# Where weights and inputs start in SBUF: one ring slot and four input quarters at other residues of 256 bytes

## What is computed

```python
def layer(x, ...):
    h = rms_norm(x, g_pre_mix)
    qA, kA, vA, qB, kB, vB = split(h @ w_in)            # 2048 x 4352
    oA = sliding_window_gqa(rope(qA), rope(kA), vA)     # window 128, with sinks
    oB = dilated_attention(rope(qB), rope(kB), vB)      # (128,1), (512,4), (2048,16)
    o = concat(rms_norm(oA, g_out_a), rms_norm(oB, g_out_b))
    x = x + rms_norm(o @ w_out, g_post_mix)             # 2048 x 2048
    h = rms_norm(x, g_pre_ffn)
    u, up = h @ w_gate, h @ w_up                        # 2048 x 5632 each
    c = conv_b + sum(conv_w[j] * shifted(u, j) for j in range(3))
    return x + rms_norm((gelu(c) * up) @ w_down, g_post_ffn)   # 5632 x 2048
```

## The kernel before

| tensor | tile step in bytes | residue of its tiles |
|---|---|---|
| `wh`, `wl`, all four slots | 512 between weight tiles | 128 |
| `hh`, `hl` | 1280 (264 columns in rows of ROW = 320) | 128, all 16 |
| `oBh`, `oBl` | 1056 | 224 + 32 j for tile j |
| `gh` | 1056 | 128 + 32 kt |
| `gl` | 1056 | 0 + 32 kt |

## Time and profile before

### The profile page before, as it was taken

One profiled execution on the slowest core, in us unless ns is written; L12 is line 12 of the kernel. 1 busy time (PEld: TensorE's weight loads), 2 busy tenths in 40 slices (PEclk: granted clock), 3 DMA queues, 4 the chain that ended last, 5 costly groups with the idle time before them and its releaser, 6 DMA issues.

```text
span 1178.7 us, 25575 instructions
## 1 busy us (share of the span) xinstructions
PE 1154.6 (98%) x9947; PEld 1122.2 (95%) x9947; DVE 700.6 (59%) x1052; ACT 552.7 (47%) x857; POOL 108.0 (9%) x163
## 2 busy tenths in 40 slices
PE   8999999999999799999999999999999999999995
PEld 8999889988999799999999999999999999999994
DVE  6977565674475866665656565665656444454445
ACT  6545555565455654444445444444545333343331
POOL 0200111111002010010001001100100000020001
PEclk9999999999999899999999999999999999999998
DMA  9646676677555345555565555546455655555542
GB/s 330 194 148 229 236 254 235 218 232 237 170 178 180 108 146 194 190 183 187 162 204 170 185 179 184 186 164 207 167 194 176 211 178 178 179 181 180 180 156 73
DMA packets 60497, 222.21 MB, mean 189 GB/s; under 512 B 7064, under 2 KB 9312, under 8 KB 58336
## 3 DMA queue, kind: packets, MB, share of 16 engines
q1 hardware_dynamic: 56032, 196.53, 51.2%
q0 software_dynamic: 4272, 24.94, 6.4%
q10 hardware_dynamic: 144, 0.05, 0.0%
HBM read 216.45 MB, written 5.00 MB: 188 GB/s over the span
## 4 chain that ended last, share of the span: by engine, by line
PE 93%; DVE 4%; ACT 1%; DMA 1%; issue 0%; SPq 0%; DVEq 0%; ACTq 0%
PE ps L1138 29%; PE ps L1139 29%; PE ps L1140 29%; DVE wl L681 1%; PE ps L1311 1%; PE ps L1229 1%; PE ps L1292 1%; DMA raw<-in_w_in 1%; PE ps L1220 1%; PE ps L1218 1%; PE ps L1247 0%; PE ps L1165 0%; DVE yT L985 0%; DVE ps L984 0%; ACT oBh L545 0%
## 5 line engine op out<-in xcount | busy, mean ns | idle before, releaser
L1138 PE MATMUL ps<-hh,wh 128*128 128x264 f32 x2080 | 593.3, 285 | 7.9 <-DVE hl L894 5.8
L1140 PE MATMUL ps<-hh,wl 128*128 128x264 f32 x2080 | 586.8, 282 | 0.0
L1139 PE MATMUL ps<-hl,wh 128*128 128x264 f32 x1952 | 550.8, 282 | 0.0
L681 DVE TENSOR_TENSOR wl<-raw,wh 128x1024 fp32r<-128x1024 f32 x363 | 438.5, 1225 | 184.4 <-ACT wh L425 183.9
L425 ACT CAST wh<-raw 128x1024 fp32r<-128x1024 f32 x363 | 374.7, 1046 | 270.3 <-PE ps L1140 268.7
L1138 PEld LDWEIGHTS ps<-hh,wh 128*128 128x128 f32 x2080 | 390.9, 188 | 20.0 <-issue 16.9
L1140 PEld LDWEIGHTS ps<-hh,wl 128*128 128x128 f32 x2080 | 390.9, 188 | 0.0
L1139 PEld LDWEIGHTS ps<-hl,wh 128*128 128x128 f32 x1952 | 367.0, 188 | 0.1
L1139 PE MATMUL ps<-gl,wh 128*128 (+1 forms) x704 | 200.4, 285 | 0.0
L1138 PE MATMUL ps<-gh,wh 128*128 (+1 forms) x704 | 200.1, 284 | 0.0
L1140 PE MATMUL ps<-gh,wl 128*128 (+1 forms) x704 | 199.5, 283 | 0.0
(11 more groups left out here) (230 smaller groups left out, 833.9 us busy)
## 6 DMA issues: line engine op xcount, KB each, us to landing
raw<-in_w_gate SPq DMA_DIRECT2D x88, 512.0 KB, 3.7
raw<-in_w_up SPq DMA_DIRECT2D x88, 512.0 KB, 4.6
raw<-in_w_down SPq DMA_DIRECT2D x88, 512.0 KB, 3.6
raw<-in_w_in SPq DMA_DIRECT2D x67, 512.0 KB, 4.8
raw<-in_w_out SPq DMA_DIRECT2D x32, 512.0 KB, 3.8
Kt<-in_kb POOLq DMA_DIRECT2D x8, 1284.0 KB, 6.5
Vk<-in_vb POOLq DMA_DIRECT2D x8, 1024.0 KB, 7.1
out_y<-yT SPq DMA_DIRECT2D x8, 264.0 KB, 2.3
```

The lines of the kernel that those rows point to most:

```text
L681: V.tensor_tensor(wl[:, slot], raw[:, slot], wh[:, slot].bitcast(F32), ALU.subtract).then_inc(lo_ready, 1)
L1138: nc.tensor.matmul(out, a, x, start=start, stop=False)
L1139: nc.tensor.matmul(out, a, xl, start=False, stop=False)
L1140: return nc.tensor.matmul(out, b, x, start=False, stop=stop)
```

## The change

The rings `wh` and `wl` are no longer one tensor of four slots each but four tensors each, and `hh` and `hl` become four tensors of four tiles (quarters). Between them stand tensors `shift0`, `shift1`, ... that nothing reads or writes. They only move the addresses of what is allocated after them. `wh[slot]` and `tile(x, j)` take the place of the old slices everywhere.

```diff
-        wh = sb("wh", [P, RING, CH], F32R)
-        wl = sb("wl", [P, RING, CH], F32R)
+        shifts = []
+
+        def shift(words, into=ctx):
+            shifts.append(sb(f"shift{len(shifts)}", [P, words], F32, into))
+
+        shift(96)
+        wh = [sb("wh0", [P, CH], F32R)]
+        shift(32)
+        wh += [sb(f"wh{c}", [P, CH], F32R) for c in range(1, RING)]
+        wl = [sb(f"wl{c}", [P, CH], F32R) for c in range(1, RING)]
+        shift(96)
+        wl.insert(0, sb("wl0", [P, CH], F32R))
...
-        sb("align", [P, 16])
+        def quarters_of(name, order, into):
+            out = [None] * 4
+            for q, words in order:
+                if words:
+                    shift(words, into)
+                out[q] = sb(name + str(q), [P, 4, ROW], F32R, into)
+            return out
+
+        def tile(x, j):
+
+            return x[j // 4][:, j % 4, 0:TOK]
+
+        shift(16)
         with ExitStack() as over:
-            hh = sb("hh", [P, MT, ROW], F32R, over)[:, :, 0:TOK]
+            hh = quarters_of("hh", ((0, 0), (1, 0), (2, 16), (3, 32)), over)
         ysq = sb("ysq", [P, MT, ROW])[:, :, 0:TOK]
-
+        shift(48)
+
+        shift(16)
         with ExitStack() as over:
-            hl = sb("hl", [P, MT, ROW], F32R, over)[:, :, 0:TOK]
+            hl = quarters_of("hl", ((0, 0), (1, 0), (2, 16), (3, 32)), over)
         yT = sb("yT", [P, MT, ROW])[:, :, 0:TOK]
+        shift(48)
...
-                a, b = wh[:, slot, c:c + P], wl[:, slot, c:c + P]
+                a, b = wh[slot][:, c:c + P], wl[slot][:, c:c + P]
                 nc.tensor.matmul(out, a, x, start=start, stop=False)
                 nc.tensor.matmul(out, a, xl, start=False, stop=False)
                 return nc.tensor.matmul(out, b, x, start=False, stop=stop)
...
-                        ins = mm3(ps[:, bank + m, 0:TOK], (slot, 256 * k + P * m), xh[:, kt0 + k], xl[:, kt0 + k],
+                        ins = mm3(ps[:, bank + m, 0:TOK], (slot, 256 * k + P * m), tile(xh, kt0 + k), tile(xl, kt0 + k),
                                   first and k == 0, last and k == 3)
...
-                    gemm(chunk(0, 0, 4, n), 2 * (gi % 2), oBh, oBl, 4 * c, c == 0, c == 1)
+                    gemm(chunk(0, 0, 4, n), 2 * (gi % 2), (oBh[:, 0:4], oBh[:, 4:8]), (oBl[:, 0:4], oBl[:, 4:8]), 4 * c, c == 0, c == 1)
...
-                        gemm(chunk(B_OUTB, i, 4, 2 * g + c), 2 * ((G_IN + G_OUT + g) % 2), hh, hh[:, OT:2 * OT],
+                        gemm(chunk(B_OUTB, i, 4, 2 * g + c), 2 * ((G_IN + G_OUT + g) % 2), hh[0:2], hh[2:4],
                              4 * c, c == 0, c == 1, o2_ready)
```

More of the change, by code:

```diff
@@ L424, in split @@
                     act.wait_ge(weights_used, n - (RING - 1))
-                nc.scalar.copy(wh[:, slot], raw[:, slot]).then_inc(hi_ready, 1)
+                nc.scalar.copy(wh[slot][:], raw[:, slot]).then_inc(hi_ready, 1)
             def free_misc(ins):
@@ L543, in stage @@
                         act.wait_ge(o_normed, OT * X + j + 1)
-                        dst = hh[:, j] if X else oBh[:, j]
+                        dst = tile(hh, j) if X else oBh[:, j]
                         nc.scalar.activation(dst, oT[X][:, j], ACT.Copy,
@@ L556, in high @@
                 for j in range(*X_PARTS[c]):
-                    nc.scalar.activation(hh[:, j], xT[:, j], ACT.Copy,
+                    nc.scalar.activation(tile(hh, j), xT[:, j], ACT.Copy,
                                          scale=par[:, C_GPM + j:C_GPM + j + 1]).then_inc(xh_ready, 1)
@@ L564, in _ @@
             act.wait_ge(half_landed, 16)
-            nc.scalar.copy(wh[:, 0, 0:CH // 2], raw[:, 0, 0:CH // 2]).then_inc(half_hi, 1)
+            nc.scalar.copy(wh[0][:, 0:CH // 2], raw[:, 0, 0:CH // 2]).then_inc(half_hi, 1)
             high(1)
             act.wait_ge(raw_landed[0], 16)
-            nc.scalar.copy(wh[:, 0, CH // 2:CH], raw[:, 0, CH // 2:CH]).then_inc(hi_ready, 1)
+            nc.scalar.copy(wh[0][:, CH // 2:CH], raw[:, 0, CH // 2:CH]).then_inc(hi_ready, 1)
             split(chunk(0, 0, 4, 1))
@@ L680, in split @@
                 dve.wait_ge(hi_ready, n + 1)
-                V.tensor_tensor(wl[:, slot], raw[:, slot], wh[:, slot].bitcast(F32), ALU.subtract).then_inc(lo_ready, 1)
+                V.tensor_tensor(wl[slot][:], raw[:, slot], wh[slot][:].bitcast(F32), ALU.subtract).then_inc(lo_ready, 1)
             def wide(x, n=2):
@@ L832, in stage @@
                         dve.wait_ge(oh_ready, OT * X + j + 1)
-                        hi, lo = (hh[:, j], hh[:, OT + j]) if X else (oBh[:, j], oBl[:, j])
+                        hi, lo = (tile(hh, j), tile(hh, OT + j)) if X else (oBh[:, j], oBl[:, j])
                         V.scalar_tensor_tensor(lo, oT[X][:, j], par[:, C_GOUT + 8 * X + j:C_GOUT + 8 * X + j + 1],
@@ L843, in low_x @@
                     dve.wait_ge(xh_ready, j + 1)
-                    V.scalar_tensor_tensor(hl[:, j], xT[:, j], par[:, C_GPM + j:C_GPM + j + 1],
-                                           hh[:, j].bitcast(F32), ALU.mult, ALU.subtract).then_inc(xl_ready, 1)
+                    V.scalar_tensor_tensor(tile(hl, j), xT[:, j], par[:, C_GPM + j:C_GPM + j + 1],
+                                           tile(hh, j).bitcast(F32), ALU.mult, ALU.subtract).then_inc(xl_ready, 1)
             low_x(0)
             dve.wait_ge(half_hi, 1)
-            V.tensor_tensor(wl[:, 0, 0:CH // 2], raw[:, 0, 0:CH // 2], wh[:, 0, 0:CH // 2].bitcast(F32),
+            V.tensor_tensor(wl[0][:, 0:CH // 2], raw[:, 0, 0:CH // 2], wh[0][:, 0:CH // 2].bitcast(F32),
                             ALU.subtract).then_inc(half_lo, 1)
@@ L852, in _ @@
             dve.wait_ge(hi_ready, 1)
-            V.tensor_tensor(wl[:, 0, CH // 2:CH], raw[:, 0, CH // 2:CH], wh[:, 0, CH // 2:CH].bitcast(F32),
+            V.tensor_tensor(wl[0][:, CH // 2:CH], raw[:, 0, CH // 2:CH], wh[0][:, CH // 2:CH].bitcast(F32),
                             ALU.subtract).then_inc(lo_ready, 1)
@@ L893, in low @@
                     dve.wait_ge(h2h_ready, j + 1)
-                    V.scalar_tensor_tensor(hl[:, j], xT[:, j], par[:, C_GPF + j:C_GPF + j + 1],
-                                           hh[:, j].bitcast(F32), ALU.mult, ALU.subtract).then_inc(h2l_ready, 1)
+                    V.scalar_tensor_tensor(tile(hl, j), xT[:, j], par[:, C_GPF + j:C_GPF + j + 1],
+                                           tile(hh, j).bitcast(F32), ALU.mult, ALU.subtract).then_inc(h2l_ready, 1)
             dve.wait_ge(yg_ready, G_OUT)
```

## The result

The changed kernel takes 1189.35 us (median of 6 runs, 1188.55 to 1193.14); the kernel before took 1183.35 us in runs beside it (6 runs, 1179.91 to 1187.59). The ratio is 1.0062, 95% interval 1.004 to 1.0084: slower by 0.6%, clear of noise and under the 1% from which the prediction counts a change as slower. The profiled execution took 1189.31 us, with a span of 1187.2 us against 1178.7 before.

What follows compares the result with a forecast made beforehand. TensorE was taken as the bound, through the pitch between matmul starts. Gate/up 10.3, input projection 3.2 and output projection's second half 0.8 us gave 1194.8 from 1180.46; with half the 4.3 us offset to the median, 1197 us, range 1181 to 1209.

Steps and rivals of the forecast that it cites:

- Differences count: In down, if input start minus weight start counts, the same eight differences recur in another order, so the change costs 0.
- The signs: Gate/up would show a four-chunk period of 2.88, 2.96, 3.00, 2.92 us and about 3855 matmuls; down's length and clock unchanged.
- absolute residues: Alternative for slot 0 in gate/up: only the input's own residue counts, costing 3.3 ns more, 2.96 us a chunk.
- The sum of the pairs, 10.0 ns a group: In gate/up, slots 0 to 3 cost 0, 3.3, 5.0 and 1.7 ns a matmul over 120.0; 10.3 us in all.
- The input projection, 3.2 us: New pairs add 7.9 ns over four chunks there, times 17 groups and 24 matmuls: 3.2 us.
- Second half of the output projection, 0.8 us: Mixed pairs of high and low parts there cost 2 ns on each of 384 matmuls: 0.8 us (0.2 to 0.8).
- The sum, 14.3 us: Gate/up 10.3, input projection 3.2 and output projection's second half 0.8, added to the profiled execution's 1180.46 us: 1194.8.
- half of the offset: The profiled execution was 4.3 us under the median; half of this was kept in forecasting 1197 us for the whole kernel.
- the likeliest case: The main forecast for the whole kernel: a sum of 9 to 19 us, time 1190 to 1204 us, chance 0.42.
- rival 1: Placement hardly acts on gate/up and the projections: sum 8.5 us, 1189 by the profile, 1191 against the median; chance 0.35.
- the line: Whole-kernel time of 1196.6 us, above which the change counts as slower, by about 1%.
- Rival 3: Pitch falls under 120.0 ns; at 117 on three quarters of 5856 matmuls, 13 us saved, 1172 us; chance 0.12.

Runs made afterwards that it cites:

- the other order: The changed kernel with all weight slots at residue 128 and input quarters at 128, 192, 0, 64: 1188.65 us beside 1180.42 for the kernel before.

## Why the prediction was right, point by point

- **The sign and the place.** Slower, through the pitch of gate/up, with nothing else moved: as forecast. 7.8 of the 8.5 us lie there.
- **Differences count.** Shown for gate/up and down: by down's chunks after, by everything on by 128 bytes (the same eight lengths), and by slot 0, whose pair costs the same at (0, 0) and at (128, 128). The forecast's 0 for down was +0.3: the same differences in another order, of which mainly the one at 64 takes longer, by 0.02 us a chunk.
- **The signs.** The period of four chunks, 2.96 us in slot 1, fewer matmuls in the stretch (3874; about 3855 was said), down's length and the clock came as written. Slot 0 at 2.88 and slot 2 at 3.00 us did not: both took 2.92 on average. For slot 0 that is neither equal differences at their best nor the 2.96 of absolute residues, and it took the repeated runs of the kernel before and the other order to place it.
- **The sum of the pairs, 10.0 ns a group.** It came to 7.8 (1.6 + 3.4 + 1.6 + 1.2), and two terms were off in opposite ways. Input at 64 was put at 5.0 from the tile at 334.05 - 333.30 of the earlier trace rows; those six matmuls stood right behind a change of pair, and the pair itself costs 0.0 when it is held. Slot 0 was put at 0 and costs 1.6, because its chunk lands in the second rhythm. The other two, 3.3 and 1.7, were right to 0.5.
- **The input projection, 3.2 us.** 0.0 against the trace of before. Two more profiles of the kernel before had 270.4 and 270.2 us there, so by those it was 1.1 to 1.3. Traces of one layout differ by as much, so the term isn't resolved beyond that. It took pitches as if the chunks ran unbroken, and it counts 17 groups where the pairs hold for 15, which would be 2.8 us.
- **Second half of the output projection, 0.8 us.** 0.7.
- **The sum, 14.3 us.** 8.5 by the profiles, 6.0 by the medians. The difference between these two is the rhythm: the profiled execution of before had 120.0 ns in gate/up, an execution in the 121.3 rhythm pays 5.3 us more, and the median lies between. So the 0.6% is measured against a kernel with two speeds. The forecast kept half of the offset between profile and median for this reason; the changed kernel lost nearly all of it: its profiled execution, 1189.31 us, is its median. Its six runs lie within 4.6 us, the six of the kernel before beside them within 7.7.
- **The point, 1197, was 7.7 us too high.** The measured time is inside the stated range, but under the likeliest case's own range (1190 to 1204), as the 8.5 us are under its 9 to 19, and it is where rival 1 put it (1189 to 1191). So direction, place and the rule of differences were right, and two of the four pair costs were not. Rival 1's 8.5 us are luck: it is 6.1 + 1.6 + 0.8 where the parts took 7.8, 0 to 1.3 and 0.7, from single costs that add up, which the pitches don't bear out. It was right that a transition may be in the six-matmul costs.
- **The chance of slower, 0.46.** It doesn't follow from its parts: if the line cuts the forecast's 0.42 near its middle, about 0.21 lie over it, not 0.33. The change stayed within 1%.
- **Rival 3** is refuted for these shapes: none of the eight differences, the same for high and low parts, has a steady pitch under 120.0.
- **The skill's rule.** "TensorE: Matmul & The Clock Gate" of the Trainium skill says that loading the next weights doesn't steal read bandwidth from the running matmul. The measurements don't fit two reads that leave each other alone: with nothing changed but where the inputs and what lies behind them start, the pitch in gate/up is 120.0, 121.0 or 123.3 ns, and it goes by the difference to the weights' start. What inside SBUF or TensorE makes it so was argued, not shown.

## What to carry to other kernels

In this kernel, which TensorE bounds and where weights are loaded beside a stream of 264 columns, the difference of the two start addresses modulo 256 bytes is a parameter worth nearly 3% of the pitch (120.0 against 123.3 ns). Try it in yours: give all chunks of a long loop one difference that is cheap (here 192, input minus weights; of the four held throughout, 128 was the dearest) and keep it across borders, since mixing even good pairs costs an entry in each chunk. Before believing a change of half a per cent, read the pitch in several profiles of the unchanged kernel, since one layout can have two rhythms. A dear difference doesn't run at its dear pitch everywhere either.

## What the runs showed that was not expected

- The same program with the same addresses runs 167 chunks at 120.0 ns in one execution and at 121.3 ns in another, 5.3 us apart in that stretch (481.2 and 486.5 us).
- Entries are long: six to eight matmuls, with single distances of up to 0.13 us, so that a mean over six tells of the change between pairs as much as of the pair.
- The price of the pair with difference 128, 3.3 to 3.4 ns, is the same for 24 matmuls in a mixed layout and for 4000 in a uniform one. Yet in the trace of the uniform one fifteen chunks of the output projection run at 120.0 ns with the same difference.
- Cutting the moving columns from 256 to 224 takes 8 ns off the steady pitch; cutting from 264 to 256, or from 224 to 192, takes off nothing.
